# Turning the modulation sums behind two FFN stages, zeros in norm gaps, and a new spread of the second block's modulation pieces

## The reference, cut to what matters

```
mod = silu(c) @ mod_w[layer] + mod_b[layer]
sh1, sc1, g1, sh2, sc2, g2 = split(mod, 6)
x = x + g1 * mixer(rms_norm(x) * (1 + sc1) + sh1)
x = x + g2 * conv_ffn(rms_norm(x) * (1 + sc2) + sh2)
```

## Time and profile before

| what | value |
|---|---|
| runs | 1650.77, 1651.62, 1657.58 us; median 1651.62 |
| profiled execution | 1647.83 us, its span 1646.0 us |
| busy | PE 1495.4 (91%), DVE 1208.4 (73%), ACT 724.2 (44%) us |
| mean granted TensorE clock | 0.956 |
| ffn 0 | PE's products from 252.6 to 457.6 us |
| norm 2, conv stage | from 458 to 593 us |
| norms 5 and 6 (after ffn 1) | 840 to 860 us |

### The profile page before, as it was taken

The page is one execution under the profiler, slowest core; times in us unless marked ns, Lnnn a source line. Parts: engine busy times, 40 slices in busy tenths (PEclk is TensorE's granted clock), DMA queues, the critical chain, the costliest instruction groups (busy, mean ns, idle before and its releaser), DMA issues.

```text
span 1646.0 us, 29088 instructions
## 1 busy us (share of the span) xinstructions
PE 1495.4 (91%) x11238; PEld 1348.5 (82%) x11238; DVE 1208.4 (73%) x1913; ACT 724.2 (44%) x949; POOL 52.1 (3%) x38
## 2 busy tenths in 40 slices
PE   4597898999989878999978899999999999899998
PEld 1484488999987668999967766889998877899997
DVE  7998647888879956888875545386666769466665
ACT  2222445444454235443444566354545442355443
POOL 2501200000000000000001000000000000000000
PEclk9698999999999989999979899999999999999999
DMA  8334827878845744878822400335554433245551
GB/s 350 128 103 166 298 99 301 316 297 309 325 163 197 275 193 184 347 294 304 301 111 103 128 14 1 130 106 202 178 185 170 164 119 103 77 149 176 182 182 51
DMA packets 55188, 307.85 MB, mean 187 GB/s; under 512 B 6631, under 2 KB 7688, under 8 KB 30984
## 3 DMA queue, kind: packets, MB, share of 16 engines
q1 hardware_dynamic: 53272, 302.40, 49.6%
q10 hardware_dynamic: 1840, 4.41, 0.9%
HBM read 304.17 MB, written 1.05 MB: 185 GB/s over the span
## 4 chain that ended last, share of the span: by engine, by line
PE 83%; DVE 9%; ACT 4%; issue 2%; DMA 2%; POOL 0%; ACTq 0%; DVEq 0%
PE bank L1845 66%; PE bank L1785 2%; PE bank L2192 2%; PE bank L2057 2%; PE bank L2042 2%; PE bank L2158 2%; DVE rstd L1244 2%; DMA arena<-in_mod_later 1%; DVE hf L1262 1%; DVE h_lo L1272 1%; PE bank L1799 1%; PE bank L2176 1%; PE bank L1811 1%; ACT w_hi L650 1%; PE bank L1896 1%
## 5 line engine op out<-in xcount | busy, mean ns | idle before, releaser
L1845 PE MATMUL bank<-h_hi,w_hi 128*128 128x256 f32 x2184 | 639.4, 293 | 64.1 <-DVE h_lo L1272 53.3
L1845 PE MATMUL bank<-h_lo,w_hi 128*128 128x256 f32 x2184 | 627.9, 287 | 0.0
L1845 PE MATMUL bank<-h_hi,w_lo 128*128 128x256 f32 x2184 | 627.4, 287 | 0.0
L1095 DVE TENSOR_TENSOR w_lo<-raw,w_hi 128x2048 fp32r<-128x2048 f32 x186 | 426.5, 2294 | 135.2 <-ACT w_hi L650 134.1
L1845 PEld LDWEIGHTS bank<-h_hi,w_hi 128*128 128x128 f32 x2184 | 428.5, 196 | 79.4 <-issue 65.8
L1845 PEld LDWEIGHTS bank<-h_lo,w_hi 128*128 128x128 f32 x2184 | 429.7, 197 | 1.1 <-issue 0.7
L1845 PEld LDWEIGHTS bank<-h_hi,w_lo 128*128 128x128 f32 x2184 | 428.9, 196 | 0.0
L650 ACT ACTIVATE w_hi<-raw 128x2048 fp32r<-128x2048 f32 x186 | 355.3, 1911 | 163.9 <-PE bank L1845 117.9
L1845 PE MATMUL bank<-a_hi,w_hi 128*128 128x256 f32 (+1 forms) x760 | 222.5, 293 | 9.9 <-DVE a_lo L1272 3.7
L1845 PE MATMUL bank<-a_lo,w_hi 128*128 128x256 f32 (+1 forms) x760 | 220.2, 290 | 0.0
L1845 PE MATMUL bank<-a_hi,w_lo 128*128 128x256 f32 (+1 forms) x760 | 220.0, 290 | 0.0
(11 more groups left out here) (265 smaller groups left out, 1486.6 us busy)
## 6 DMA issues: line engine op xcount, KB each, us to landing
raw<-in_stream SPq DMA_DIRECT2D x186, 1024.0 KB, 4.9
arena<-in_mod_stream SPq DMA_DIRECT2D x64, 768.0 KB, 6.4
arena<-in_mod_later SPq DMA_DIRECT2D x48, 512.0 KB, 6.8
raw<-in_mod_pe SPq DMA_DIRECT2D x36, 512.0 KB, 5.8
arena<-in_mod_pe SPq DMA_DIRECT2D x12, 512.0 KB, 12.6
sq<-in_bias SPq DMA_DIRECT2D x8, 256.0 KB, 7.0
x<-in_x_t ACTq DMA_DIRECT2D x1, 1024.0 KB, 9.2
arena<-in_ctx_t SPq DMA_DIRECT2D x1, 1024.0 KB, 4.9
```

Of the source, the lines that this page charges most:

```text
L1095: nc.vector.tensor_tensor(w_lo[s][:], raw[s][:], w_hi[s][:].bitcast(F32), ALU.subtract).then_inc(lo_done, 1)
L1845: ins = nc.tensor.matmul(out_, l, r, start=first and n == 0, stop=last and n == 2, **kw)
```

## The change

It does five things. The first operation's sum and the final sum of each modulation block go to a buffer of their own (`mod_keep`, 16 x 384 columns) and the second partial sum to the old ring, with no wait for PE. The turns leave the FFN loops: for ffn 0, blocks 2 to 5 go ahead of the last down chunk, 0 and 1 behind norm 2's sum, 6 to 10 behind those, 11 to 15 behind chunks 0 and 1 of cm_in; for ffn 1, 0 to 7 go behind norm 5's sum, 8 to 15 behind norm 6's. `mod_out` moves accordingly. `stay_awake` multiplies zeros: 16 products ahead of every FFN stage, 20 ahead of cm_out and of hy_in. The pieces are spread anew, with none at p = 0. Their six buffers move to the front of the arena, so pieces 0 to 5 wait for the last modulation block, and stand behind chunks 0 and 1 in SP's list.

```diff
-        LATER = FREE + START_SLOTS * HALF
+        later_w = [at(i * PM_COLS, PM_COLS) for i in range(LATER_SLOTS)]
+        MOD_KEEP = FREE + START_SLOTS * HALF
+        mod_keep = at(MOD_KEEP, MOD_BLOCKS * MOD_COLS)
...
         def later_pieces(p):
-            return range((0, 6, 14, 22, 30, 40)[p], (6, 14, 22, 30, 40, 48)[p])
+            return range((0, 0, 9, 18, 29, 40)[p], (0, 9, 18, 29, 40, 48)[p])
...
-                    if m >= LATER_SLOTS:
+                    if m < LATER_SLOTS:
+                        sp.wait_ge(sem("mod_used"), MOD_SLOTS + 2 * MOD_BLOCKS)
+                    else:
                         sp.wait_ge(sem("later_used"), m - LATER_SLOTS + 1)
...
             load_ffn(0, MB[1])
+            load_plain("cm_in", 0, 2)
             load_later(0, 6)
-            load_plain("cm_in", 0, 6)
+            load_plain("cm_in", 2, 6)
             load_later(6, 12)
             load_plain("cm_in", 6, 7)
...
-                acc = ring[b % len(ring)]
-                if b >= len(ring):
-                    dve.wait_ge(sem("mod_turned"), b - len(ring) + 1 + 3 * per)
+                part = mod_acc[b % len(mod_acc)]
+                parts = [mod_keep[:, bass.ds(k0 + 3 * MOD_COLS * per, MOD_COLS)], part[:, 1, :]]
...
+            mod_out(1, 6, "mod_b", 0, 18)
             norm(2)
...
                 if p:
                     add_taps(p - 1)
+                else:
+                    mod_out(1, 16, "mod_b", 18, 48, 2)
...
             norm(6)
+            mod_out(4, 32, "mod_b_2")
...
+            def stay_awake(n):
+                for i in range(n):
+                    nc.tensor.matmul(bank[i % 3][:], zeros[:, 0:P], zeros[:], start=True, stop=True)
+            def mod_turn(b0, blocks, dst=6):
+                for b in blocks:
+                    pe.wait_ge(sem("mod_used"), MOD_SLOTS + 2 * (b0 + b) + 2)
+                    for n in range(3 * b, 3 * b + 3):
+                        ins = nc.tensor.matmul(bank[dst][:, n:n + 1], mod_keep[:, n * P:(n + 1) * P], ones[:, 0:1], start=True, stop=True)
+                    ins.then_inc(sem("mod_turned"), 1)
...
                         up_gate(s, q, i)
-                        if b0 is not None and e:
-                            mod_turn(b0 + 1, 9 * i + 3, i, parts=1)
                         down(s - 1, q + 2, i)
-                        if b0 is not None:
-                            mod_turn(b0 + 2 * e, 9 * i + 6 * e, i, parts=1)
+                if f == 0:
+                    mod_turn(b0, range(2, 6))
                 down(10, q0 + 32, last=True)
-                if b0 is not None:
-                    mod_turn(b0 + 15, 45, parts=1)
...
             norm_sum(2)
+            mod_turn(MB[1], (0, 1))
+            mod_turn(MB[1], range(6, 11), 2)
...
                     conv_taps(p - 1)
                     later(p)
+                else:
+                    mod_turn(MB[1], range(11, 16), 2)
...
             norm_sum(5)
+            mod_turn(MB[4], range(0, 8))
             norm_sum(6)
+            mod_turn(MB[4], range(8, 16))
```

More of the change, by code:

```diff
@@ L1128, in mod_block @@
                             chain_wait(last[e])
-                        ins = nc.vector.scalar_tensor_tensor(acc[:, e, :], w, c, acc[:, e, :], ALU.mult, ALU.add)
-                    if kt == DT // 2 - 1 or kt == DT - 1 and not merge:
+                        ins = nc.vector.scalar_tensor_tensor(parts[e], w, c, parts[e], ALU.mult, ALU.add)
+                    if kt == DT // 2 - 1:
                         ins.then_inc(sem("mod_used"), 1)
@@ L1134, in mod_block @@
                         last[e] = chain.on(ins)
-                if merge:
-                    chain_wait(last[1])
-                    nc.vector.tensor_tensor(acc[:, 0, :], acc[:, 0, :], acc[:, 1, :], ALU.add).then_inc(sem("mod_used"), 1)
+                chain_wait(last[1])
+                nc.vector.tensor_tensor(parts[0], parts[0], parts[1], ALU.add).then_inc(sem("mod_used"), 1)
             more = [0]
@@ L1225, in _, with mod_out @@
             dve.wait_ge(sem("powers_ready"), 1)
-            def mod_out(l, b, name, row, first=0, last=48):
+            def mod_out(l, b, name, first=0, last=48, src=6):
                 dve.wait_ge(sem("mod_turned"), b)
-                bias = par[:, COL[name] + row + first:COL[name] + row + last]
-                link(nc.vector.tensor_tensor(mod[:, l, first:last], bank[6][:, first:last], bias, ALU.add))
+                bias = par[:, COL[name] + 48 + first:COL[name] + 48 + last]
+                link(nc.vector.tensor_tensor(mod[:, l, first:last], bank[src][:, first:last], bias, ALU.add))
             def first_mod_out(g0, g1):
@@ L1467, in run @@
                         if b0 is not None and k in blocks:
-                            mod_block(b0 + blocks[k], c0, i, merge=True)
+                            mod_block(b0 + blocks[k], c0, i)
                 g = step(0, q0)
@@ L1492, in ffn @@
                 if b0 is not None:
-                    mod_block(b0 + 15, c0, merge=True)
+                    mod_block(b0 + 15, c0)
                 for k in range(DT):
@@ L1982, in filter_layer, with ffn @@
                 nc.tensor.matmul(bank[6][0:HY_HID, 0:T], hy_w[n], (pos, hid[0])[n], start=True, stop=True).then_inc(sem("hy_mlp"), 1)
-            def ffn(f, b0):
+            def ffn(f, b0=None):
                 q0 = Q[f"ffn{f}"]
                 done = f * (FT // 2)
+                stay_awake(16)
                 for b in range(4):
@@ L2098, in _ @@
             norm_sum(LAYER_NORM)
+            stay_awake(20)
             projection("cm_out", 4, h_of(LAYER_NORM))
-            ffn(1, MB[4])
+            ffn(1)
             norm_sum(5)
+            mod_turn(MB[4], range(0, 8))
             norm_sum(6)
+            mod_turn(MB[4], range(8, 16))
             for c in range(2):
@@ L2197, in _ @@
             filter_layer(0)
-            ffn(2, None)
+            ffn(2)
             norm_sum(12)
+            stay_awake(20)
             for j in range(len(HY)):
@@ L2249, in _ @@
             projection("hy_out", 13, part_of("hy_out"))
-            ffn(3, None)
+            ffn(3)
             norm_sum(14)
```

13 lines of the change are left out of this document (5 added, 8 removed).

## The result

| what | before | after |
|---|---|---|
| median | 1651.19 us (4 runs) | 1698.88 us (4 runs, 1689.59 to 1701.24) |
| profiled execution, span | 1647.83, 1646.0 us | 1697.53, 1695.7 us |
| granted clock, mean | 0.956 | 0.945 |

The ratio is 1.0271, with a 95% interval of 1.0223 to 1.0318: slower by 47.7 us. The forecast was 1689, and the time lies in its range of 1672 to 1708.

The account below looks back on a forecast made before the run. TensorE products were taken as the first bound, with two stages close to VectorE. Terms -15.6 + 1.4 + 53 + 1.5 - 2.3 = +38.0 us gave 1689.6 from a 1651.6 median, forecast as 1689, range 1672 to 1708.

Parts of the forecast that it names:

- FFN loops: ffn 0 and ffn 1: 12 turns leaving PE's loop gain 7.8 us per stage, -15.6 us for two.
- Norm 2: Norm 2's reciprocal queues behind the new mod_out, which waits for turns 0 and 1 on PE: +1.4 us.
- The conv stage: Weight chunks held behind waiting pieces in SP's list, plus lower clock: +53 us, from 44 to 58.
- The term +6 for the clock: Conv stage: three PE restarts at low clock after long waits, about +6 us, ends 0 and +10.
- the holds: Conv stage: chunks issued late behind pieces in SP's list make the mean start 46.8 us later.
- Norms 5 and 6: ffn 1's turns placed behind the two norm sums overfill PE's gaps: +1.5 us, ends -1.2 and +9.
- eight turns take 5.4 us: Norms 5 and 6: length of each group of turns on PE, against gaps of 4.00 and 5.28 us.
- Zeros: Zero products ahead of FFN stages, cm_out and hy_in gain little, VectorE pacing first chunks: -2.3 us, ends 0 and -2.3.
- the rule of full return: Rival: zeros at six starts give back length times missing clock, 13.1 us in all; total 1679, chance 0.07.
- The weights were held up: Denies the rival that conv-stage chunks 6 to 9 land in time, stage paying 2.6 us; total 1639, chance 0.06.
- the first hold only: Rival: in the conv stage later pairs catch up, +10.5 in place of 53; total 1647, chance 0.04.
- The low clock: Rival: one-column products don't hold the clock; conv 58, norms 5 and 6 +9, zeros nothing; total 1706, chance 0.13.

Follow-up runs that it names:

- Number 11: Kernel before the change, with the three one-column products of each modulation block issued twice; 1678.31 us, ratio 1.0153.
- number 1: Changed kernel, with every conv-stage weight chunk ahead of the pieces it doesn't need in SP's list; 1655.0 us, ratio 1.0012.
- number 2: Changed kernel, with chunk 6 alone moved ahead of pieces 6 to 11 in SP's list; 1685.52 us (one run).
- number 5: Changed kernel, with only the old spread of the later pieces put back; 1636.23 us, ratio 0.9912.
- number 8: Changed kernel, with 60 products of zeros ahead of the turns of the first three later sums in the conv stage; 1697.51 us, ratio 1.0270.
- number 9: Changed kernel with the old spread and without any products of zeros; 1640.87 us, ratio 0.9933.
- number 3: Kernel before the change, with the new spread of the pieces alone; 1710.41 us (one run).
- number 6: Changed kernel with eight buffers for pieces, spread 4, 8, 8, 8, 12, 8, a matching transfer list, and ffn 1's blocks turned in three places; 1626.1 us, ratio 0.9834.
- number 4: Kernel before the change, with the products of zeros alone added; 1649.95 us, ratio 0.9979.
- number 10: number 6 with norm 3's sum ahead of four last pieces and the turn, ACT's copy behind the root, those twenty zeros out; 1622.18 us, ratio 0.9825.

## Why the prediction was right, point by point

**FFN loops.** Forecast -7.8 each, measured -6.9 with norm 2's 1.07 us included, so -8.0, and -8.3. Number 11 shows the 0.67 us a turn as the price of added products. In the traces of numbers 1, 2, 5, 8 and 9, which have the same FFN code but for number 9's missing zeros, the two stretches became 5.4 to 6.4 and 5.9 to 8.3 us shorter, so this trace is at or above the upper end of them and the closeness of -8.0 to -7.8 is in part luck.

**Norm 2.** Forecast +1.4, measured +1.1 (0.61 to 1.68 us behind the sum), with the wait where it was said: behind `mod_out` on VectorE.

**The conv stage.** The mechanism was right: SP issues chunk 6 at 500.07, past six pieces; ACT's hi idles 19.34, 33.38 and 33.76 us; VectorE 11.38, 18.60 and 19.34; PE 13.83, 17.68 and 16.37. Numbers 1, 3 and 5 put all of it on the spread against the list. The size was off by 8.1 us: 61.1 lies above the 44 to 58 given for this stage. The later starts of taps were forecast at +10.5, +27.4 and +43, and came at +11.9, +32.5 and +52.0; the mean came at +59.6 instead of +46.8. Those forecasts are at the full clock; the lower clock stood beside them as +6. In the pair shown by the chain, 46.1 us from chunk products to chunk products instead of the 42.0 forecast, the transfer is the 12.4 that I had. Of the other 4.1, 2.6 are work of PE that ran in part at half clock: products at 12.65 (the 96 ahead of the rows shown) instead of 11.7, and the turn with two pieces in 3.7 instead of 2.0. The pieces up to SP's issue of the next ones took 3.5 instead of 1.9, and ACT's part was 0.2 shorter. From the taps of p = 3 to the mean it was 27.9 us instead of 24.0: 2.3 more up to the end of conv taps 3, with a turn and five pieces at half clock in 5.4 us, and 1.5 more for the eleven pieces behind (11.0 instead of 9.5). The term +6 for the clock, with ends 0 and +10, was of the right kind: at most 9.0 us in the three stretches (number 8). What is left for the holds is then 50.6 us or more where I had 46.8, so that term was mis-sized too, by 3.8 us at the least.

**Norms 5 and 6.** Forecast +1.5 with ends of -1.2 and +9, measured +6.2. The step that failed is "eight turns take 5.4 us": they took 7.93 and 8.04. Turns of one column did not keep the clock up in this run. In number 5 the same code cost +2.0, and in number 6, with fewer of them in each gap, +0.6.

**Zeros.** Forecast -2.3. The change has -2.5 in its three stretches, number 4 measures -3.5 (0.0021 x 1651; -2.0 by the medians). That the rule of full return, 13.1 us, would not hold was right.

**The rivals.** The weights were held up (number 1 against number 3), so 1639 is out, and so is the first hold only, 1647 (number 2). The low clock came true in part. The conv stage took 61.1, nearer to its 58 than to my 53, and norms 5 and 6 took +6.2, nearer to its +9 than to my +1.5; norm 2 (+1.1) and the zeros (-2.5) came as I had them and not as it had them. The measured 1698.88 is 9.9 us above the forecast and 7.1 below that rival's 1706. The direction and the mechanism of the loss were right; that the number fell in the range owes something to the range, which reaches up to this rival. By the terms listed for it the range would be 1678 to 1706, so its lower end of 1672 is 6 us lower than they give.

## What to carry to other kernels

A list of transfers with waits in it is part of every schedule that it feeds. Whoever moves the first use of a buffer later must look at what stands behind that buffer's next load: here one line of a spread held SP, with 1 MB chunks behind it, for up to 39 us at a time and cost 61 us, and with the spread back the same change is 0.9% faster than the kernel before. Where work is spread over gaps, a gap takes as many pieces for their compute time as there are buffers; each one more costs its transfer (1.27 us instead of 0.46). Before a gap is filled with zeros, see whether real work that now stands ahead of the critical sum can fill it (number 10: 8 us within the stage).

## What the runs showed of the hardware that I had not expected

- Half clock over 58.1 us of a stage cost at most 9.0 us, since PE worked for only 17.9 of them. 180 products of zeros in its waits, 39 us of PE (13.1 each), left the ratio at 1.027: the clock was at 1.00 under the zeros and at 0.50 for 12.9 us of the work that followed.
- Two groups of 48 records of one-column products, back to back with a sum, ran at 0.66 and 0.65 of the clock in one program and at 0.75 and 0.95 in another that differs from it in the spread of the pieces alone. Whether such products hold the clock is thus not settled: in neither run did they hold it throughout. The Trainium skill (TensorE: Matmul & The Clock Gate, Part 1) calls the ramp run-variable. One trace for each program cannot show that; in line with it, the mean granted clock over the ten executions of number 1 was between 0.952 and 0.960.
